# First slab of a stage on the scaled input, with the norm's token factor and shift applied at its read-out

## The reference

```python
def modulate(x, g, shift, scale):
    return rms_norm(x, g) * (1 + scale[:, None, :]) + shift[:, None, :]
e = silu(c @ cond_w + cond_b)
for i in range(2):
    mod = (e @ ada_w[i] + ada_b[i]).reshape(B, 3, 3, D)   # shift, scale, gate of three sublayers
    shift, scale, gate = mod[:, :, 0], mod[:, :, 1], 1 + mod[:, :, 2]
    h = modulate(x, norm_g[i, 0], shift[:, 0], scale[:, 0])
    x = x + 0.5 * gate0 * ((silu(h @ w1) * (h @ w3)) @ w2)
    h = modulate(x, norm_g[i, 1], shift[:, 1], scale[:, 1])
    x = x + gate1 * (conformer_conv(h) if i == 0 else stick_breaking_attention(h))
    h = modulate(x, norm_g[i, 2], shift[:, 2], scale[:, 2])
    x = x + 0.5 * gate2 * ((silu(h @ w1) * (h @ w3)) @ w2)
```

## Time and profile before

| | us |
|---|---|
| median of 3 runs (2159.23 to 2163.16) | 2160.94 |
| the profiled execution | 2158.89 |
| its span, first to last instruction | 2157.1 |
| PE busy in the span | 2080.7 (96%) |
| DVE, ACT, POOL busy | 1095.1, 664.2, 247.4 |
| mean granted clock | 0.98 |

### The profile page before, as it was taken

The page is one execution under the profiler, slowest core; times in us unless marked ns, Lnnn a source line. Parts: engine busy times, 40 slices in busy tenths (PEclk is TensorE's granted clock), DMA queues, the critical chain, the costliest instruction groups (busy, mean ns, idle before and its releaser), DMA issues.

```text
span 2157.1 us, 24244 instructions
## 1 busy us (share of the span) xinstructions
PE 2080.7 (96%) x9556; PEld 1675.0 (78%) x9556; DVE 1095.1 (51%) x1240; ACT 664.2 (31%) x744; POOL 247.4 (11%) x145
## 2 busy tenths in 40 slices
PE   5999999999899999999999999999999899999999
PEld 5888888766578888888788888866878777888887
DVE  7655554477956555522655432254469834333222
ACT  2332322232344223222432222232157633222221
POOL 1100001121211000011100000110025511000000
PEclk9999999999899999999999999999989999999999
DMA  8444442434423445433344323322100022222222
GB/s 325 166 184 168 193 177 113 178 102 125 131 78 137 175 175 194 153 104 109 123 194 171 130 74 103 106 88 78 59 1 1 30 88 78 94 82 95 86 94 92
DMA packets 45414, 261.80 MB, mean 121 GB/s; under 512 B 6416, under 2 KB 7056, under 8 KB 20528
## 3 DMA queue, kind: packets, MB, share of 16 engines
q1 hardware_dynamic: 42288, 256.84, 32.5%
q10 hardware_dynamic: 3072, 4.23, 0.8%
HBM read 250.49 MB, written 2.10 MB: 117 GB/s over the span
## 4 chain that ended last, share of the span: by engine, by line
PE 89%; DVE 4%; issue 2%; DMA 2%; ACT 2%; POOL 1%; SPq 0%; DVEq 0%; POOLq 0%; ACTq 0%
PE ps L1207 27%; PE ps L1209 26%; PE ps L1208 26%; PE ps L1228 3%; PE ps L1512 2%; PE ps L1235 1%; DMA stage<-ada_d 1%; ACT w L540 1%; PE ps L1392 1%; DMA raw<-down_d 1%; DVE act_tmp L777 1%; DVE w L764 1%; PE ps L1433 1%; PE ps L1289 1%; DVE ada_acc L777 0%
## 5 line engine op out<-in xcount | busy, mean ns | idle before, releaser
L1207 PE MATMUL ps<-h_hi,w 128*128 128x512 f32 x1680 | 670.9, 399 | 1.4 <-DVE h_lo L1166 1.4
L1208 PE MATMUL ps<-h_lo,w 128*128 128x512 f32 x1680 | 662.6, 394 | 0.0
L1209 PE MATMUL ps<-h_hi,w 128*128 128x512 f32 x1680 | 662.5, 394 | 0.0
L1207 PEld LDWEIGHTS ps<-h_hi,w 128*128 128x128 f32 x1680 | 315.8, 188 | 84.5 <-issue 9.1
L1209 PEld LDWEIGHTS ps<-h_hi,w 128*128 128x128 f32 x1680 | 315.6, 188 | 79.2
L1208 PEld LDWEIGHTS ps<-h_lo,w 128*128 128x128 f32 x1680 | 315.8, 188 | 73.6
L764 DVE TENSOR_TENSOR w<-raw,w 128x1408 fp32r<-128x1408 f32 (+1 forms) x100 | 187.8, 1878 | 243.7 <-ACT w L540 243.6
L540 ACT ACTIVATE w<-raw 128x1408 fp32r<-128x1408 f32 (+1 forms) x100 | 156.9, 1569 | 470.8 <-PE ps L1209 404.0
L1207 PE MATMUL ps<-g_hi,w 128*128 128x512 f32 x704 | 274.6, 390 | 2.4 <-DVE w L764 2.3
L1209 PE MATMUL ps<-g_hi,w 128*128 128x512 f32 x704 | 274.0, 389 | 0.0
L1208 PE MATMUL ps<-g_lo,w 128*128 128x512 f32 x704 | 273.9, 389 | 0.0
(11 more groups left out here) (187 smaller groups left out, 1960.9 us busy)
## 6 DMA issues: line engine op xcount, KB each, us to landing
raw<-up_d SPq DMA_DIRECT2D x88, 1024.0 KB, 6.2
ada_raw<-ada_d SPq DMA_DIRECT2D x64, 1024.0 KB, 4.8
raw<-down_d SPq DMA_DIRECT2D x64, 704.0 KB, 4.1
raw<-mix_d SPq DMA_DIRECT2D x28, 1024.0 KB, 4.8
stage<-ada_d SPq DMA_DIRECT2D x12, 1024.0 KB, 13.1
u_blk<-u SPq DMA_DIRECT2D x64, 64.5 KB, 2.1
u_blk<-u ACTq DMA_DIRECT2D x64, 64.5 KB, 2.1
x<-x_t_d SPq DMA_DIRECT2D x2, 1024.0 KB, 18.2
```

Of the source, the lines that this page charges most:

```text
L1207: pe.matmul(dst, a_hi_, b_hi_, start=start, stop=False, skip_group_check=True)
L1208: pe.matmul(dst, a_hi_, b_lo_, start=False, stop=False, skip_group_check=True)
L1209: return pe.matmul(dst, a_lo_, b_hi_, start=False, stop=stop, skip_group_check=True)
```

## The change

It touches five entries, m = 1 (conv), 3, 4, 6 (feed-forward 1, 2, 3) and 5 (QKV). Since the token factor is one number per token and the shift one per feature, h @ w = factor * ((x * gain) @ w) + shift @ w. The first slab of these stages multiplies x times the gain column, split into high and low parts chunk by chunk behind each x_add (`entry_high` on ACT, `entry_low` on DVE; in tiles of their own for m = 3 and 6, else in h's). The norm's sums and spread move into that slab, after chunks 2 and 5. shift @ w of this slab comes from eight DVE operations on the raw slab (`shift_sums`) and two one-column matmuls (`bias_sums`). h is still made as before, for all other slabs, and the second slab takes its chunks as they come. At the read-out DVE copies the factor row, multiplies both banks by it, and the bias is added in Silu, in the sigmoid or by DVE. The split of the second slab's weights now stands ahead of h, not behind it.

```diff
@@ ACT
+            def entry_high(m, c):
+
+                if c == 0:
+                    act.wait_ge(gs_done, (m if m < 2 else m - 1) + 1)
+                act.activation(entry(m)[0][:, c, :], x[:, c, :], ACT.Copy, scale=gs[:, c:c + 1]).then_inc(ehi_done, 1)
+                    if m and entry(m)[0] is h_hi:
+                        if c < KD - 1:
+                            act.wait_ge(e_used, (KD - 1) * ENTRY[m] + c + 1)
+                        else:
+                            act.wait_ge(slab_done, FIRST[m] + 1)
...
+                tmp = act_tmp[:, s, :]
+                if first:
+                    tmp = up_tmp[0]
+                    act.wait_ge(u0_done, 2 * ENTRY[first] + 1)
+                    act.wait_ge(bias_done, ENTRY[first] + 1)
+                    act.activation(tmp, tmp, ACT.Silu, bias=b0[:, 0:1]).then_inc(silu_done, 1)
+                else:
+                    act.wait_ge(slab_done, n + 1)
+                    act.activation(tmp, pair[s][0], ACT.Silu).then_inc(silu_done, 1)
...
                     if not last:
                         square(m, d, x[:, d, :], x_done, KD * max(0, m - 2) + d + 1)
+                        entry_high(m, d)
...
             for c in range(KD):
+                if c == 0:
+                    act.wait_ge(u0_done, 1)
+                    act.wait_ge(bias_done, 3)
+                    act.activation(prod[:, 0, :], prod[:, 0, :], ACT.Sigmoid, bias=b0[:, 1:2]).then_inc(sig_done, 1)
@@ DVE
+            def entry_low(m, c):
+
+                dve.wait_ge(ehi_done, KD * ENTRY[m] + c + 1)
+                e = entry(m)
+                dve.scalar_tensor_tensor(out=e[1][:, c, :], in0=x[:, c, :], scalar=gs[:, c:c + 1],
+                                         in1=f32(e[0][:, c, :]), op0=ALU.mult, op1=ALU.subtract).then_inc(elo_done, 1)
+
+            def shift_sums(m):
+
+                n = FIRST[m]
+                dve.wait_ge(raw_s[0], 16 * (n // 2 + 1))
+                for k in range(KD):
+                    src, w = raw[0][:, 2 * k * P:2 * (k + 1) * P], mod(*MODS[m], 0, k, 1)
+                    if k == 0:
+                        dve.tensor_scalar(shift_acc, src, w, None, ALU.mult).then_inc(shift_step, 1)
+                    else:
+                        dve.wait_ge(shift_step, KD * ENTRY[m] + k)
+                        dve.scalar_tensor_tensor(out=shift_acc, in0=src, scalar=w, in1=shift_acc, op0=ALU.mult,
+                                                 op1=ALU.add).then_inc(shift_step, 1)
...
+            def first_factor(m, dst, src):
+
+                if src is pair[0][0] or src is pair[0][1]:
+                    dve.wait_ge(slab_done, FIRST[m] + 1)
+                dve.wait_ge(fac_kept, ENTRY[m] + 1)
+                return dve.tensor_tensor(dst, src, ss[:, :], ALU.mult)
+
+            def h_lows(m, layer, sub):
+
                 if m:
                     factor(m)
+                    lo(FIRST[m] + 1)
+                    keep_bias(m)
...
+                if m:
+                    dve.tensor_copy(ss[:, :], row).then_inc(fac_kept, 1)
...
+                tmp = act_tmp[:, s, :]
+                if first:
+                    tmp = up_tmp[0]
+                    first_factor(first, up_tmp[0], pair[0][0]).then_inc(u0_done, 1)
+                    first_factor(first, up_tmp[1], pair[0][1]).then_inc(u0_done, 1)
+                    dve.wait_ge(silu_done, f + 1)
+                    dve.wait_ge(u0_done, 2 * ENTRY[first] + 2)
+                    dve.scalar_tensor_tensor(out=tmp, in0=up_tmp[1], scalar=b0[:, 1:2], in1=tmp, op0=ALU.add,
+                                             op1=ALU.mult).then_inc(g_full, 1)
+                else:
+                    dve.wait_ge(silu_done, f + 1)
+                    dve.tensor_tensor(tmp, tmp, pair[s][1], ALU.mult).then_inc(g_full, 1)
...
                 for d in range(KD):
                     if d < KD - 1:
                         lo(N_DOWN[j] + 2 * d + 2, DOWN)
                     elif not last:
+                        if m:
+                            shift_sums(m)
                         lo(nxt)
+                    if m and d >= 1:
+                        entry_low(m, d - 1)
                     dve.wait_ge(slab_done, N_DOWN[j] + 2 * d + 2)
                     x_add(d, down_ps[d % 2])
...
+                if m:
+                    entry_low(m, KD - 1)
...
             h_lows(1, 0, 1)
-            lo(N_CONV + 1)
...
+            first_factor(1, prod[:, 0, :], pair[0][1]).then_inc(u0_done, 1)
+            first_factor(1, prod[:, 1, :], pair[0][0]).then_inc(u0_done, 1)
...
                 elif i == 2:
+                    shift_sums(3)
                     lo(N_UP[1])
...
                     x_add(2 * i + b, pair[i % 2][b])
+                    if i or b:
+                        entry_low(3, 2 * i + b - 1)
...
+                if s == 0:
+                    for b in range(2):
+                        first_factor(5, qk[:, b, :], pair[0][b]).then_inc(u0_done, 1)
+                        dve.wait_ge(u0_done, 2 * ENTRY[5] + b + 1)
+                        dve.tensor_scalar(qk[:, b, :], qk[:, b, :], b0[:, b:b + 1], None, ALU.add).then_inc(qk_done, 1)
@@ PE
+            def first_slab(m):
+
+                hi_, lo_ = entry(m)
+                w = wsp[0]
+                if m in (3, 6):
+                    pe.wait_ge(x_done, KD * (m - 2) + KD - 2)
+                for k in range(KD):
+                    if k == 2:
+                        sums(m)
+                    if k == 5:
+                        spread(m)
+                        bias_sums(m)
+                    pe.wait_ge(ehi_done, KD * ENTRY[m] + k + 1)
+                    pe.wait_ge(elo_done, KD * ENTRY[m] + k + 1)
+                    for b in range(2):
+                        at = slice((2 * k + b) * P, (2 * k + b + 1) * P)
+                        last = triple(pair[0][b], w[:, 0, at], w[:, 1, at], hi_[:, k, :], lo_[:, k, :],
+                                      k == 0, k == KD - 1)
+                    if k < KD - 1:
+                        last.then_inc(e_used, 1)
+                return last
+
+            def bias_sums(m):
+
+                pe.wait_ge(shift_step, KD * (ENTRY[m] + 1))
+                if m in (1, 4):
+                    pe.wait_ge(mod_done, (Q_DOWN + 2 if m == 1 else Q_FFN[1] + 10) + 1)
+                for b in range(2):
+                    last = pe.matmul(bias_ps[:, b:b + 1], shift_acc[:, b * P:(b + 1) * P], ones[:, 0:1], start=True,
+                                     stop=True, skip_group_check=True)
+                last.then_inc(bias_sum, 1)
...
-            stats(1)
...
+                if c == 0:
+                    first_slab(1).then_inc(slab_done, 1)
+                    return
```

More of the change, by code:

```diff
@@ L160, in trunk @@
             con = ov("con", [P, 4, P], F32R)
+        with ExitStack() as scope:
+            ov("pad_e", [P, 4 * SLAB])
+            e_hi = ov("e_hi", [P, KD, S], F32R)
+            e_lo = ov("e_lo", [P, KD, S], F32R)
+            ov("pad_f", [P, 2 * (KF - KD) * S - 2 * S])
+            up_tmp = [ov(f"up_tmp{i}", [P, S])[:, :] for i in range(2)]
         with ExitStack() as scope:
@@ L222, in trunk @@
         hsum_done = sem("hsum_done")
+        ehi_done = sem("ehi_done")
+        elo_done = sem("elo_done")
+        e_used = sem("e_used")
+        shift_step = sem("shift_step")
+        bias_sum = sem("bias_sum")
+        bias_done = sem("bias_done")
+        fac_kept = sem("fac_kept")
+        u0_done = sem("u0_done")
         h_done = sem("h_done")
@@ L320, in ss_steps, with entry @@
             return 6 * m
+        def entry(m):
+            return (e_hi, e_lo) if m in (3, 6) else (h_hi, h_lo)
+        shift_acc = act_tmp[:, 1, 0:2 * P]
+        bias_ps = ps[:, 7, 16:18]
         def t_buf(c):
@@ L573, in h_his, with up_step @@
                         act.activation(h_hi[:, c, :], t_buf(c), ACT.Identity, bias=shift).then_inc(hhi_done, 1)
-            def up_step(j, i, s, split=True, ada=False):
+            def up_step(j, i, s, split=True, ada=False, first=None):
                 n = N_UP[j] + 2 * i + s
@@ L591, in ffn @@
                 for s in range(2):
-                    up_step(j, 0, s)
+                    up_step(j, 0, s, first=FFN_ENTRY[j] if s == 0 else None)
                 if nb:
@@ L886, in ffn @@
                     for s in range(2):
-                        up_step(j, 0, s, True, take=False)
+                        up_step(j, 0, s, True, take=False, first=FFN_ENTRY[j] if s == 0 else None)
+                elif FFN_ENTRY[j]:
+                    for s in range(2):
+                        up_step(j, 0, s, False, first=FFN_ENTRY[j] if s == 0 else None)
+                if nb:
                     with dve.Fori(1, min(nb, 10)) as i:
@@ L891, in ffn @@
                 if nb < 10:
-                    with dve.Fori(nb, 10) as i:
+                    with dve.Fori(max(nb, 1), 10) as i:
                         for s in range(2):
@@ L991, in _ @@
```

(11 more changed lines are left out.)

78 lines of the change are left out of this document (48 added, 30 removed).

## The result

The changed kernel takes **2124.8 us** (median of four runs, 2122.1 to 2129.6) against 2160.7: a ratio of 0.9835, 95% interval 0.9815 to 0.9856. The profiled execution is the slowest of the four, 2129.6 us with a span of 2127.8, so the two profiled executions are 29.3 us apart.

What follows compares the result with a forecast made beforehand. TensorE, busy 96% of the span, was taken as the bound, so only its idle time and slow stretches could be won. Terms 5.1+4.6+6.5+7.5-2.2-1.5-2.5 = 17.5 us gave 2143.4 us against the median, range 2136 to 2153.

Steps and rivals of the forecast that it cites:

- the sum: Whole kernel: the terms add to 17.5 us gained, taken from the profiled execution's 2158.9 us.
- first down phase: First feed-forward's down phase: entry_low stands in a loop of DVE, SP, DMA and ACT without cover, costing 2.5 us.
- conv branch: Conv entry m=1: taps start no earlier, and after 7.5 us idle run on the slow clock, costing 1.5 us.
- m=3: Feed-forward 1 entry: slab 3 starts at T+27.4 instead of T+32.55, a gain of 5.1 us.
- m=4: Feed-forward 2 entry: gain of 4.6 us, with an ada reduction ahead of the slab shifting the chain.
- m=5: QKV entry: no stall before slab 3, which starts at T+27.0 instead of T+34.5, a gain of 7.5 us.
- m=6: Feed-forward 3 entry: gain of 6.5 us from a window of 22.8 us.
- The clock behind the stalls: PE after new 2.3 us stalls before slab 3: half of 1.5 us charged at three places, costing 2.2 us.
- All cover holds: Rival: clock stays up at stalls and after the conv wait, DVE's loop swallows entry_low; 23.7 us gained, 2137; 12%.
- The read-out: Rival: the first slab's read-out costs more, lengthening the stall before slab 3; 10 us less gain, 2153; 16%.
- the norm's chain: Rival: chain late inside the first slab, PE stops 3 us at the spread; 15 us less gain, 2158; 7%.
- GpSimd beside DVE: Rival: h chain and read-out on DVE slowed beside GpSimd, 6 us late at five entries; slower, 2173; 7%.

Runs made afterwards that it cites:

- e2: The kernel before with one unused tile of 8 bytes a partition ahead of st, no instruction touched: 2141.6 us, ratio 0.992.
- e1: The changed kernel with b0 put into two unused columns of st, so in the old layout with the same instructions: 2141.4 us, ratio 0.9912.
- e3: The changed kernel with only the conv entry (m=1) put back to the old form: 2116.5 us.
- e4: The changed kernel with slab 3's weight split put ahead of the first read-out's remaining steps at the three feed-forward entries: 2115.3 us.
- d1: The kernel before with 8 unused bytes ahead of x, the first tile, so all tiles move together: 2156.3 us.
- d2: The kernel before with 72 unused bytes ahead of x, the first tile, so all tiles move together: 2157.4 us.
- l4: The kernel before with 8 unused bytes a partition between raw0 and w0: 2147.8 us.
- l5: The kernel before with 24 unused bytes ahead of st: 2152.6 us.
- l6: The kernel before with 72 unused bytes ahead of st: 2130.3 us.
- c_pad64: The changed kernel with conv entry put back and early split of slab 3's weights, plus 64 more unused bytes: 2102.3 us, ratio 0.9736.

## Why the prediction was wrong

**The step that failed is the sum.** It added the steps to a program whose other slabs were taken to stay as they were ("A slab at full speed takes 11.2 us"). They did not: the pace of all slabs fell to 10.99 through b0's 8 bytes, worth 17.8 us (e2). In the prediction b0 has no line, since it costs no time to declare a tile. Without it the changed kernel stands at 2141.4 us (e1), where 2143.4 was forecast, inside the range. That these two are so near is in part luck, as the terms below show.

**Term by term**, from e1 against the kernel before, both at 11.20, by the stage times in the table:

| term | forecast | measured |
|---|---|---|
| first down phase | -2.5 | -2.9 (after against e2: -2.7) |
| conv branch | -1.5 | -5.3; by the means over profiles -2.9 |
| m=3, with its share of the clock | 5.1-0.7 | 5.3 |
| m=4, same | 4.6-0.7 | 3.1 |
| m=5 | 7.5 | 7.9, and about 3 more at the end of the stage, within its scatter |
| m=6, same | 6.5-0.7 | 5.2 |

The measured column adds to 16.3, as the two profiled executions do (2158.9 and 2142.8, 16.1 apart). With the mean for the conv branch and without the 3 at the end of attention it is 15.7, so the steps gave somewhat less than the 17.5 forecast; at the medians e1 is 18.0 below the kernel before.

*First down phase.* Right in kind and size; the waits for the split in the down phases grew from 2.3 to 4.2 us.

*Conv branch.* Right in kind: idle 8.48 us against 7.5, the taps start at T+34.3 against T+33.3. The chain of waits of the changed kernel:

```profile
459.82 1.14 DVE u L1121
...
465.79 3.39 DMA u_blk<-u
469.32 7.44 PE ps L1570 x40
```

The first u starts at T+24.8 as forecast (25.0), and the restacks are issued 6.0 us later, as forecast; the last lands after 3.4 us where I had 2.1, the median of all 64 in the earlier trace rows. The window of the taps behind the wait:

```profile
469.30:475.00 5.70, 5.68 (x28) 1.57 (x32) 4.22 (x5) 2.52 (x2) 0.00 (x0) 0.50 0.60 193
```

The clock is at 0.50 from the first tap on, and the first forty take 7.44 us. I had 5.85 for that from the earlier trace rows; against the 4.43 of the earlier trace rows it is 3.0 lost, not 1.4. With 1.0 for the later start the term is 4.0, where 1.5 were forecast: mis-sized by 2.5.

*The clock behind the stalls.* Charged at 2.2, spread evenly over three places, it cost 3.2 at two of them and nothing at the third. Behind 2.26 us of idle at m=3 the granted clock is 1.00; behind 2.28 at m=4 and 2.26 at m=6 it is 0.54 and 0.52 in the windows shown, and each lost 1.6. e1 has the same pattern (idle 2.07, 2.01 and 2.07; clock kept at m=3, lost at m=4 and 6), and so does e3. The term was right in kind and mis-sized by 1.0, and it accounts for the other rows of the table: 5.1, 4.6-1.6 and 6.5-1.6 are 5.1, 3.0 and 4.9, where 5.3, 3.1 and 5.2 were measured. Why m=3 keeps its clock behind a stall of the same length stays open. The Trainium skill, TensorE: Matmul & The Clock Gate, "Why this matters for your kernels", asks only that longer gaps be avoided, and by that rule the sum would have been 19.7; the trace agrees with it at m=3 and not at m=4 and m=6, and there the measurement decides.

*m=5.* PE's first matmul of the attention scores, by the tile's rows (durations, first and last start), before:

```profile
L1207 PE MATMUL ps<-qk_s x64: 217/437/792, 1581.9 to 1711.6; 64*128 64x384 f32 x16, 64*128 64x128 f32 x16, 64*128 64x256 f32 x16, 64*128 64x512 f32 x16
```

and e1 (T=1406.6):

```profile
L1347 PE MATMUL ps<-qk_s x64: 217/437/792, 1573.9 to 1703.4; 64*128 64x384 f32 x16, 64*128 64x128 f32 x16, 64*128 64x256 f32 x16, 64*128 64x512 f32 x16
```

T+175.2 becomes T+167.3, a gain of 7.9. The rest comes behind the last score matmul, where 64.6 us become 61.8, and is not shown to be work of the change. e2, without any of it, has 61.0 there. From the first score matmul to the last x_add of the stage the thirteen profiles with the old steps take 190.4 to 196.8 us (mean 193.8) and the seven with the new ones 190.5 to 194.1 (mean 192.2), so the 3 us lie within the scatter. Behind the last score matmul the granted clock falls below 1 in twelve of the thirteen and in two of the seven; whether the change has a part in that stays open.

**The rivals.** None of them came. "All cover holds" (2137) failed in all that it asked: the clock fell at two of the three stalls and behind the conv wait, and the first down phase lost its 2.9 us. The read-out, the norm's chain and GpSimd beside DVE cost what the forecast case had. All four were rivals about the steps, and none asked what else a new tile does.

## What to carry to other kernels

A tile that is declared moves all tiles behind it, and here that alone was worth as much as the steps of the change. Before an edit is credited or blamed, compare in both traces the pace of work that it doesn't touch (here two read-outs of one slab), and run the old instructions in the new layout and the new ones in the old. In a kernel bound by TensorE, try a few unused bytes between the moving tiles and the weight tiles, each pair of them by itself, and measure rather than align. And where the first slab's read-out has become longer, send the weight split that the slab after next waits for ahead of the rest of it (e4).

## What the runs showed of the hardware that I had not expected

- The same 48 matmuls (128x128 by 512 columns, operands declared float32r, back to back, granted clock 1.00) take 10.88, 10.99 or 11.20 us, up to 3% apart, by the distance in the partition between the weight tile and the tile that streams against it; 66 down matmuls take 14.96 or 15.40 in the same way. Moving both together changes nothing (d1, d2). From the distance of the kernel before, 8, 16 and 24 bytes more are faster, 72 fastest, 40, 56 and 104 like 0. Which distances are good, and by what conflict, stays open.
- At the distances of 10.99 a whole feed-forward can run at 11.20 (feed-forward 3 in the profiles of the changed kernel, l4 and l5); at that of 72 bytes neither profile has it (l6, c_pad64). What switches it stays open.
- Idle times of PE of one length don't have one price. In the changed kernel 2.26 us ahead of slab 3 left the granted clock at 1.00 at m=3, and 2.28 and 2.26 us at m=4 and m=6 were followed by a stretch near 0.5 that cost 1.6 us; e1 and e3 repeat it place by place. What decides it stays open.
- Of the eight 128x256 products of DVE the first (TENSOR_SCALAR) took 1.38 to 1.39 us at four entries and 0.35 at the conv entry; why it is so long at four of them stays open. The seven behind it took 0.49 each on the average, near the 0.47 that I took. Timeline of DVE in the changed kernel:

```profile
625.93 1.38 DVE L905 TENSOR_SCALAR act_tmp<-raw,mods 128x256 f32<-128x256 f32 x1
627.35 3.61 DVE L908 SCALAR_TENSOR_TENSOR act_tmp<-raw,mods,act_tmp 128x256 f32<-128x256 f32 x7
```
